# A state-space layer's sample state update: one product of 96 stacked rows instead of four full-precision strips

## The reference

```python
xdt = (xh * dt[..., None]).reshape(bsz, nc, q, GROUPS, HPG, HEADDIM)
states = jnp.einsum('bclgn,bcgrl,bclgrp->bcgrpn', bc, jnp.exp(cs[..., -1:] - cs), xdt)
h_last = h0 * jnp.exp(cs[..., -1]) + states      # samples: one chunk of 4 tokens
```

## Time and profile before

| | |
|---|---|
| median of 3 runs | 1655.26 us (1651.9 to 1657.22) |
| the profiled execution | 1650.94 us |
| its span on the core | 1649.2 us |
| PE busy | 1475.4 us (89%) |
| DVE busy | 1067.4 us (65%) |
| ACT busy | 715.7 us (43%) |
| POOL busy | 599.6 us (36%) |
| mean granted TensorE clock | 0.933 of full speed |

### The profile page before, as it was taken

The page is one execution under the profiler, slowest core; times in us unless marked ns, Lnnn a source line. Parts: engine busy times, 40 slices in busy tenths (PEclk is TensorE's granted clock), DMA queues, the critical chain, the costliest instruction groups (busy, mean ns, idle before and its releaser), DMA issues.

```text
span 1649.2 us, 33844 instructions
## 1 busy us (share of the span) xinstructions
PE 1475.4 (89%) x12754; PEld 1340.3 (81%) x12754; DVE 1067.4 (65%) x2293; ACT 715.7 (43%) x1352; POOL 599.6 (36%) x681
## 2 busy tenths in 40 slices
PE   5998989999999997869899999999999789888985
PEld 4887978887777774748799999999998689788885
DVE  4788671455655665565757778867977454668856
ACT  1676342343443444332534445444544322367632
POOL 1545434222221120125334435444544445245541
PEclk6999979999999999979779999999999799799998
DMA  3222243666657566522132324323332132032221
GB/s 114 78 73 68 69 121 93 186 196 201 197 171 223 176 185 203 184 81 64 44 85 57 105 56 119 103 66 109 103 105 83 42 101 88 29 107 72 66 72 64
DMA packets 282539, 179.75 MB, mean 109 GB/s; under 512 B 18906, under 2 KB 280826, under 8 KB 282376
## 3 DMA queue, kind: packets, MB, share of 16 engines
q1 hardware_dynamic: 282376, 177.58, 36.4%
HBM read 160.67 MB, written 16.86 MB: 108 GB/s over the span
## 4 chain that ended last, share of the span: by engine, by line
PE 62%; DVE 22%; ACT 6%; issue 5%; SPq 2%; DMA 1%; POOL 1%; ACTq 0%; DVEq 0%; POOLq 0%
PE proj_lo L1627 11%; PE proj L1627 11%; PE proj_lo L197 6%; PE proj L197 4%; PE proj_lo L871 3%; PE proj L871 3%; PE r L882 2%; DVE conv L476 2%; PE x L966 2%; PE s L1674 2%; DVE rms L1305 2%; PE s L894 1%; DVE h L525 1%; DVE h L530 1%; DVE g L534 1%
## 5 line engine op out<-in xcount | busy, mean ns | idle before, releaser
L172 POOL TENSOR_TENSOR w_low<-w_raw,w_high 128x256 fp32r<-128x256 f32 x608 | 535.1, 911 | 952.1 <-ACT w_high L163 952.0
L163 ACT ACTIVATE w_high<-w_raw 128x1024 fp32r<-128x1024 f32 x152 | 160.0, 1053 | 151.7 <-PE proj_lo L1627 50.8
L1627 PE MATMUL proj<-xh,w_high 128*128 128x288 f32 x440 | 138.1, 314 | 0.0
L1627 PE MATMUL proj<-xh,w_low 128*128 128x288 f32 x440 | 132.6, 301 | 0.0
L1627 PE MATMUL proj<-xl,w_high 128*128 128x288 f32 x440 | 132.1, 300 | 0.0
L1627 PE MATMUL proj_lo<-xh,w_high 128*128 128x256 f32 x440 | 130.6, 297 | 0.0
L1627 PE MATMUL proj_lo<-xl,w_high 128*128 128x256 f32 x440 | 127.2, 289 | 0.0
L1627 PE MATMUL proj_lo<-xh,w_low 128*128 128x256 f32 x440 | 126.2, 287 | 0.0
L1627 PEld LDWEIGHTS proj_lo<-xh,w_high 128*128 128x128 f32 x440 | 86.6, 197 | 11.0 <-issue 11.0
L1627 PEld LDWEIGHTS proj<-xh,w_high 128*128 128x128 f32 x440 | 86.0, 195 | 1.8 <-issue 1.5
L1627 PEld LDWEIGHTS proj_lo<-xl,w_high 128*128 128x128 f32 x440 | 86.5, 197 | 0.0
(11 more groups left out here) (472 smaller groups left out, 4438.5 us busy)
## 6 DMA issues: line engine op xcount, KB each, us to landing
k_pages<-in_cache_k SPq DMA_DIRECT2D x256, 128.0 KB, 2.4
v_pages<-in_cache_v SPq DMA_DIRECT2D x256, 128.0 KB, 2.3
w_raw<-in_c_in_w SPq DMA_DIRECT2D x48, 512.0 KB, 3.9
w_raw<-in_a_in_w SPq DMA_DIRECT2D x32, 512.0 KB, 4.0
w_raw<-in_b_in_w SPq DMA_DIRECT2D x32, 512.0 KB, 4.2
w_raw<-in_a_out_w SPq DMA_DIRECT2D x16, 512.0 KB, 4.0
st<-in_state_ssd_h SPq DMA_DIRECT2D x16, 512.0 KB, 5.1
out_ssd_h_sample<-st SPq DMA_DIRECT2D x16, 512.0 KB, 5.6
```

The costliest lines, as they stand in the source:

```text
L163: act.activation(k.wh[par][:], k.raw[par][:], ACT.Copy).then_inc(k.sem["w_hi"], 1)
L172: step = pool.tensor_tensor(k.wl[par][:, tiles, :], k.raw[par][:, tiles, :], k.wh[par][:, tiles, :], ALU.subtract)
L1627: mm = pe.matmul(out, w[par][:, i, :], x[:, i, cols], start=first and opens and i == 0 and n == 0, stop=last and i == KT - 1 and n == 2, s ...
```

## The change

The samples' four strips become one product over 96 partitions, again four instructions of 512 columns each, but in fp32r. Partitions 0 to 31 hold the high part of the decayed x, 32 to 63 its low part, 64 to 95 the high part again; against them stand the high part of B twice and its low part once. So the three partial products of high and low are summed inside the array. DVE makes the parts: `decayed` keeps the prompt's four chunks alone, and a new function `state_parts` is called in step n = 2, behind `results`.

```diff
-            rows, j, half = slice(NS * q, NS * q + NS), q // 2, q % 2
+        pe.wait_ge(sem["state_parts"], g + 1)
+        rows = slice(0, 3 * NS)
...
-            pe.matmul(c_out(k, bank, "state", g, q), k.xdd[rows, QB, j * P:j * P + P], k.bm[rows, 4 * half:4 * half + 4, :],
+            pe.matmul(c_out(k, bank, "state", g, q), k.xdd_r[rows, QB, j * P:j * P + P], k.bm[rows, 4 * half:4 * half + 4, :],
                       start=True, stop=True).then_inc(sem[f"c{bank}_done"], 1)
...
-        dve.tensor_tensor(k.xdd[:].rearrange("p c (r q) -> p c r q", r=HPG), k.xtok[g % 2][:].rearrange("p c (r q) -> p c r q", r=HPG),
-                          k.dec[:, :, heads].unsqueeze(3).broadcast_to([P, CH, HPG, HD]), ALU.mult)
-        dve.tensor_tensor(k.bm, k.btok[:, QB:CH, :].broadcast_to([P, NB, STATE]),
-                          k.blk[:, 0:NS:DT].unsqueeze(2).broadcast_to([P, NB, STATE]), ALU.mult).then_inc(sem["xdd_ready"], 1)
+        dve.tensor_tensor(k.xdd[:, 0:QB].rearrange("p c (r q) -> p c r q", r=HPG),
+                          k.xtok[g % 2][:, 0:QB].rearrange("p c (r q) -> p c r q", r=HPG),
+                          k.dec[:, 0:QB, heads].unsqueeze(3).broadcast_to([P, QB, HPG, HD]), ALU.mult).then_inc(sem["xdd_ready"], 1)
+
+    def state_parts(g):
+
+        high, low, tokens = slice(0, 3 * NS), slice(NS, 2 * NS), slice(2 * NS, 3 * NS)
+        scratch = k.bm[tokens, 0, :]
...
+        decayed_samples(k.xdd_r[high, QB, :], high)
+        decayed_samples(k.fresh[low, :], low)
+        dve.tensor_copy(scratch, k.btok[tokens, QB, :]).then_inc(sem["state_in"], 1)
+        dve.wait_ge(sem["state_in"], 2 * g + 1)
+        dve.tensor_tensor(k.xdd_r[low, QB, :], k.fresh[low, :], k.xdd_r[low, QB, :], ALU.subtract)
+        dve.tensor_tensor(k.btok[tokens, QB, :], k.btok[tokens, QB, :], scratch, ALU.subtract).then_inc(sem["state_in"], 1)
+        dve.wait_ge(sem["state_in"], 2 * g + 2)
+        dve.tensor_tensor(k.bm[high], k.btok[high, QB:CH, :].broadcast_to([3 * NS, NB, STATE]),
+                          k.blk[high, 0:NS:DT].unsqueeze(2).broadcast_to([3 * NS, NB, STATE]), ALU.mult).then_inc(sem["state_parts"], 1)
...
                     results(u, n - 1)
+                    if n == 2:
+                        state_parts(u)
```

More of the change, by code:

```diff
@@ L110, in allocate @@
     k.gh, k.gl = k.g[:, 0:KT, :], k.g[:, KT:2 * KT, :]
+    with nc.sbuf_tensor("sq_parts", [P, 2, T], F32R) as k.sq_r:
+        pass
     k.sq = [sb(f"sq{j}", [P, 2, T]) for j in range(2)]
@@ L139, in allocate @@
         c_ready o_squared b_head
-        c_params c_taps c_consts dt_raw adt_ready a_exp dec_in dt_made st_landed st_ready st_out hout_ready hp_out
+        state_in state_parts c_params c_taps c_consts dt_raw adt_ready a_exp dec_in dt_made st_landed st_ready st_out hout_ready hp_out
         g_squared g_made g_ready g_high g_split acc_added ctails_turned ctails_read ctails_out y_in feat_ready
@@ L1458, in layer_c_buffers @@
     k.sz = [[sz[0], sz[2]], [sz[1], sz[2]]]
+    k.xdd_r = k.view("xdd_parts", [P, CH, 2 * P], F32R)
     k.xdd = k.sb("xdd", [P, CH, 2 * P])
@@ L1470, in layer_c_buffers @@
     k.ctails = k.sb("c_tails", [P, CONV_C // P, HN])
-    k.bm = k.sq[0].rearrange("p a t -> p (a t)")[:, 0:NB * STATE].rearrange("p (b n) -> p b n", b=NB)
+    k.bm = k.sq_r.rearrange("p a t -> p (a t)")[:, 0:NB * STATE].rearrange("p (b n) -> p b n", b=NB)
+    k.fresh = k.sq[0].rearrange("p a t -> p (a t)")[:, 0:2 * P]
     def old_states(place):
@@ L1755, in new_states @@
             c_may_fill(pe, k, "s" if q < 2 else "r", "state", g, q)
+        pe.wait_ge(sem["state_parts"], g + 1)
+        rows = slice(0, 3 * NS)
         for q in range(4):
-            rows, j, half = slice(NS * q, NS * q + NS), q // 2, q % 2
+            j, half = q // 2, q % 2
             bank = "s" if q < 2 else "r"
-            pe.matmul(c_out(k, bank, "state", g, q), k.xdd[rows, QB, j * P:j * P + P], k.bm[rows, 4 * half:4 * half + 4, :],
+            pe.matmul(c_out(k, bank, "state", g, q), k.xdd_r[rows, QB, j * P:j * P + P], k.bm[rows, 4 * half:4 * half + 4, :],
                       start=True, stop=True).then_inc(sem[f"c{bank}_done"], 1)
@@ L2166, in decayed, with decayed_samples @@
         heads = slice(HPG * g, HPG * g + HPG)
-        dve.tensor_tensor(k.xdd[:].rearrange("p c (r q) -> p c r q", r=HPG), k.xtok[g % 2][:].rearrange("p c (r q) -> p c r q", r=HPG),
-                          k.dec[:, :, heads].unsqueeze(3).broadcast_to([P, CH, HPG, HD]), ALU.mult)
-        dve.tensor_tensor(k.bm, k.btok[:, QB:CH, :].broadcast_to([P, NB, STATE]),
-                          k.blk[:, 0:NS:DT].unsqueeze(2).broadcast_to([P, NB, STATE]), ALU.mult).then_inc(sem["xdd_ready"], 1)
+        dve.tensor_tensor(k.xdd[:, 0:QB].rearrange("p c (r q) -> p c r q", r=HPG),
[4 more added lines that the diff above has]
+        scratch = k.bm[tokens, 0, :]
+        def decayed_samples(out, rows):
+            n = rows.stop - rows.start
+            decay = k.dec[rows, QB, HPG * g:HPG * g + HPG].unsqueeze(2).broadcast_to([n, HPG, HD])
+            return dve.tensor_tensor(out.rearrange("p (r q) -> p r q", r=HPG),
+                                     k.xtok[g % 2][rows, QB].rearrange("p (r q) -> p r q", r=HPG), decay, ALU.mult)
+        decayed_samples(k.xdd_r[high, QB, :], high)
[7 more added lines that the diff above has]
+                          k.blk[high, 0:NS:DT].unsqueeze(2).broadcast_to([3 * NS, NB, STATE]), ALU.mult).then_inc(sem["state_parts"], 1)
     def finish(g):
@@ L2625, in scoped, with view @@
 def scoped(nc, k, make):
+    def view(name, shape, dtype):
+        with nc.sbuf_tensor(name, shape, dtype) as t:
+            return t
     with ExitStack() as ctx:
         k.sb = lambda name, shape, dtype=F32: ctx.enter_context(nc.sbuf_tensor(name, shape, dtype))
+        k.view = view
         make(k)
```

## The result

The changed kernel takes 1668.2 us (median of 4 runs, 1664.52 to 1668.39), the kernel before 1654.2 us on the same chip (4 runs): a ratio of 1.0092, 95% interval 1.0074 to 1.0109. It is 0.9% slower. The forecast was 1682 us and 1.6%; the time lies within its range, near the lower end. The profiled execution took 1664.52 us, its span is 1662.5 us.

A forecast was written before the change was run, and what follows sets the result against it. PE sets the pace, DVE arriving just after it at chunk 4's weights. Profiled 1650.9 + 20.3 (seven stages) + 2.7 (last stage) - 0.8 (product) + 5 (clock) = 1678.1 us; median 4.3 higher, 1682 us, range 1665 to 1697.

The forecast's parts named there:

- What bounds the kernel, and step 0: PE sets the pace; taking 2.0 us from DVE's step 0 gains nothing, its wait growing from 0.95 to about 3 us.
- Six instructions, 3.1 us (2.7 to 3.3): DVE's added work in step n = 2 takes 3.1 us, after four joints give back 0.36 us.
- a margin of 0.35 us to either side: DVE work shifted out of POOL's way gains, or work shifted into it loses, up to 0.35 us.
- Two new waits: PE waits 0.9 us at `prompt_state` and 2.3 us at the old states; each full stage 2.9 us longer, seven 20.3 us.
- The last stage, 2.7 us: PE already waits at `prompt_state` in the last stage, so no slack: 2.7 us longer (2 to 3.2).
- The product, 0.1 us a stage: Four new products on PE at most 0.94 us against 1.07: gain 0.1 us in each of 8 stages, 0.8 us.
- The rival in which the strips hold PE four times as long: Old strips take PE four times the new ones' time, so 2.8 us a stage come off: 1660 us; 2%.
- The clock, +5 us: PE's new waits may each bring a half-clock dip costing 0 to 1.7 us: 5 of 11.7 us; old dips unchanged.
- its first rival: No new wait drops PE's clock and some old dips are missed: 1672 us, 1666 with delay at its lower bound; 15%.
- The rival of the POOL lock: In step 2, POOL blocks DVE for a whole instruction, 0.6 to 1.7 us a stage: 1686 to 1694 us; 12%.

The follow-up runs named there:

- the run with the old product: Kernel before with its four fp32 strips, samples' multiplications moved from step 0 to step 2 and filled up to six fp32 instructions on 128 partitions: 1669.54 us, ratio 1.012.
- mask_twice: Changed kernel with the last of its six instructions (masked B, 1024 elements) made twice in step 2, the second waiting for the first: 1685.11 us, ratio 1.0202.
- The last experiment: Changed kernel with its six instructions in step 5 and the samples' outputs in two separate runs of 32 products: 1640.84 us, ratio 0.9945 to the kernel before.

## Why the prediction was right, and what was mis-sized

1. *What bounds the kernel, and step 0.* Right. What left step 0 became idle time (2.90 us, 3 forecast), and moving it out alone gains nothing (0.9981 to 1.0023).
2. *Six instructions, 3.1 us (2.7 to 3.3).* 3.43 us, above the range. The forecast took 0.09 us for each of four joints from a row in which both instructions use all partitions. Three of them gave back nothing, since the next instruction starts at another partition; the fourth, to the feature, gave 0.07. That alone is the 0.3 us. The last one took 1.65 us where 1.76 was at the upper end. That chunk 3's weights came 3.1 us late all the same, as forecast, is luck: the feature's 0.5 us more and the convolution's 0.8 us less stood in the forecast only as a margin of 0.35 us to either side.
3. *Two new waits.* Right: 0.99 us (0.9) and 2.07 (2.3), both for the weights. A plain stage grew by 2.66 us; the forecast had 2.9, less 0.1 for the product. Seven stages: 18.6 us.
4. *The last stage, 2.7 us.* Too little: 3.6 us more wait at `prompt_state` (4.20 and 0.58). The six take 3.62 us there: the first takes 1.04 instead of 0.42 us beside POOL instructions (two of them, 3.12 us from 1303.43 on) that the forecast had not looked for.
5. *The product, 0.1 us a stage.* 0.13 us. The four take 1.03 us (919.97 to 921.00) against 1.07, and the second product of slot 5's low half now starts 0.12 us after the first (921.00 to 921.12); before it was 0.23 us (922.04 to 922.27). The expected 0.85 to 0.95 us was too little, and what is gained lies in good part behind the four. The rival in which the strips hold PE four times as long falls with this.
6. *The clock, +5 us.* This is the term that was mis-sized, and its sign was wrong: -4.6 us over the six stages. Two steps of it failed. The new waits were to bring dips that cost up to 1.7 us each. In three of the seven stages a stretch does begin some 1.2 us behind the wait at `prompt_state`, but it is taken in by the second wait and costs nothing; none followed the wait of 2.1 us. And the old dips were set at no change; they went from five to two. The forecast had named the price of this case in its first rival, at 1672 us, though with no new dips at all.

The account of the profiled executions closes. From the layer's first sums (870.01 us before, 866.21 after) to the last stage's four products it comes to 18.6 + 3.5 (the last stage) - 4.6 = 17.5 us, and the trace has 444.33 us before and 461.84 after. What lies ahead of these sums, which the change does not touch, took 3.8 us less in the profiled run of the changed kernel; that leaves 13.7 us, and 13.6 lie between the two profiled times. The forecast had 27.2 us between them. Of the 9.7 us between 27.2 and 17.5 nearly all is the clock; the 3.8 us ahead of the layer belong to these two executions, and whether the medians have them is not shown.

The rival of the POOL lock was priced from a low part of 1.1 us, a fourth of the row of four. That is not its length when it runs by itself, which the first line gives (shortest, median and longest of all 608, in ns); the other two are the first two of the four that the last of the six instructions meets in the changed kernel:

```profile
L174 POOL TENSOR_TENSOR w_low<-w_raw,w_high x608: 718/741/1795, 9.1 to 1633.3; 128x256 fp32r<-128x256 f32 x152
...
1012.45 0.76 POOL L174 TENSOR_TENSOR w_low<-w_raw,w_high 128x256 fp32r<-128x256 f32 x1 [4.86 <-ACT w_high L165]
1013.17 1.71 POOL L174 TENSOR_TENSOR w_low<-w_raw,w_high 128x256 fp32r<-128x256 f32 x1
```

The multiplication begins at 1012.64 us, when POOL's first has 0.57 us to go, and takes 1.65 us: 0.43 more than the 1.22 of the last stage, where no POOL instruction runs beside it. POOL's second takes 1.71 us and ends at 1014.88, 0.59 us behind the multiplication. In the run with the old product, where the multiplication begins 0.09 us ahead of POOL, it takes 1.23 us, and POOL's first takes 1.74. So each waits for all but the last 0.15 us or so of the other's instruction. The Trainium skill, SBUF — State Buffer, section Who interferes with whom, calls the ports that the two share an exclusive lock, and says that the order of issue decides who blocks; the trace agrees. The forecast took the lock to cost up to a whole 1.1 us, and took L2169's 1.765 us at most to speak against it. Both were misread: the multiplication waits only for what is left of one POOL instruction of 0.74 us, and the 1.76 us of the earlier trace rows already had such a wait in it.

What stays open is why the stretches begin where they do. In the kernel before they begin 58.0 us apart in six successive stages (977.5 to 1267.6 us); in the changed one, with stages of 58.95 us, they come in pairs 119.5 us apart. One could say that a stage of another length meets them more seldom, but in `mask_twice` a stage of another length again meets them more often, so that this gives no rule to forecast with. All of these counts come from one execution of each kernel, and the kernel before ran at mean granted clocks of 0.932 to 0.950 in 19 executions on one chip (1642.3 to 1656.2 us), so that others may have other counts. The last experiment points to the run of 64 small products: halved, they are gone from all six stages, and the median of ten runs is lower too (a ratio of 0.9945 to the kernel before, against 0.9982 with the parts in step 5 alone). That the length of the run is the cause is not shown, since the halves also change the length of the stage and the order on PE.

## What to carry to other kernels

Slack belongs to a place: find, for each place where work can go, how long its engine idles before the next thing that another engine must hand it; the same six instructions, with the new product, cost 2.7 us a stage in step 2, 0.65 in step 0, and nothing in step 5. Moving work out of a place with slack gains nothing. And before a clock term is given a sign, see which stretches at half clock there are now, and in which a wait stands close behind that would take one in.

## What the runs showed of the hardware

- A run of 64 products of 4 columns, 2.0 us with PE always busy, stands ahead of half-clock stretches of 3.4 us that cost 1.5 us, in five of six stages of the kernel before; two runs of 32, 1.1 us each and 3.3 us apart, stand ahead of none in six stages. Spread in eights among large products, behind a PE wait of 2.0 us, the same 64 lie in stretches of 13.7 to 17.1 us at a clock of 0.50 to 0.53 in five of six stages.
- A half-clock stretch ahead of a wait for another engine is taken in by it: the wait shrank from 2.07 to 0.56 us.
- Successive VectorE instructions that wait for nothing start 0.07 to 0.09 us before the one ahead ends when both start at the first partition, whether they use 32, 96 or 128 of them, and do not when the next one starts at another partition (0.43 us apart at 0.42 us of length, where it was 0.33).
- VectorE's multiplication of two SBUF operands and POOL's low part, 1.22 and 0.74 us long by themselves, take turns: begun with 0.57 us of POOL's left, the multiplication took 1.65 us; begun 0.09 us ahead of POOL's, it took 1.23, and POOL's 1.74. So a 0.41 us multiplication took 0.88 us beside POOL and a 0.22 us cast 0.67.
- Four fp32 products of 32 rows beside one another (1.07 us) and four fp32r products of 96 rows one after another (1.03 us) take PE nearly the same time.
